# High parts subtracted in PSUM by TensorE, and two bias loads issued later, in a hybrid attention and expert layer

## The reference

```
gu = xe @ w_gu[e] + b_gu[e]                    # 1024 -> 2048
gate = min(gu[..., 0::2], 7); up = clip(gu[..., 1::2], -7, 7)
act = (up + 1.0) * (gate * sigmoid(gate * 1.702))
y = act @ w_dn[e] + b_dn[e]                    # 1024 -> 1024
out[row] += y * row_gate
```

## Time and profile before

| | |
|---|---|
| runs | 1425.9, 1427.1, 1428.12 us; median 1427.1 |
| profiled execution | 1428.16 us, span 1426.5 us |
| busy over the span | TensorE 93%, weight load 74%, VectorE 89%, ScalarE 72%, GpSimd 31% |
| transfers | 472.83 MB, mean 331 GB/s |
| TensorE clock | 0.99 of full speed over the span |

### The profile page before, as it was taken

One profiled execution on the slowest core, in us unless ns is written; L12 is line 12 of the kernel. 1 busy time (PEld: TensorE's weight loads), 2 busy tenths in 40 slices (PEclk: granted clock), 3 DMA queues, 4 the chain that ended last, 5 costly groups with the idle time before them and its releaser, 6 DMA issues.

```text
span 1426.5 us, 20070 instructions
## 1 busy us (share of the span) xinstructions
PE 1331.1 (93%) x6410; PEld 1058.9 (74%) x6410; DVE 1276.3 (89%) x1246; ACT 1026.1 (72%) x945; POOL 439.6 (31%) x286
## 2 busy tenths in 40 slices
PE   6999989898999999999999999999999999999996
PEld 5876866776877777787877777777878777788883
DVE  7448665689999999999999999999999999999998
ACT  5344444447788888878788888888787888877772
POOL 0000000023143536253444435362535444311100
PEclk9999999999999999999999999999999999999998
DMA  9511130279999999999999999999999999999994
GB/s 352 192 59 60 35 133 31 83 264 382 378 395 403 402 393 406 409 403 405 406 406 400 402 394 404 397 401 406 403 398 400 408 397 396 390 380 374 364 372 178
DMA packets 85573, 472.83 MB, mean 331 GB/s; under 512 B 16619, under 2 KB 16659, under 8 KB 34336
## 3 DMA queue, kind: packets, MB, share of 16 engines
q1 hardware_dynamic: 70736, 451.79, 79.6%
q0 software_dynamic: 14800, 20.55, 4.1%
HBM read 467.80 MB, written 22.02 MB: 343 GB/s over the span
## 4 chain that ended last, share of the span: by engine, by line
PE 50%; DVE 22%; issue 13%; DMA 7%; ACT 6%; POOL 0%; DVEq 0%; SPq 0%; POOLq 0%; ACTq 0%
DVE w_lo L1004 11%; PE gu_bank L1536 10%; PE gu_bank L1538 9%; PE gu_bank L1537 9%; DMA raw<-in_w_down_dram 5%; ACT w_hi L645 4%; PE turn_bank L1536 3%; PE turn_bank L1537 3%; PE turn_bank L1538 3%; DVE arena L1384 2%; PE bank L1536 1%; PE bank L1538 1%; PE bank L1537 1%; PE bank L1861 1%; DVE arena L1394 1%
## 5 line engine op out<-in xcount | busy, mean ns | idle before, releaser
L1004 DVE TENSOR_TENSOR w_lo<-raw,w_hi 128x2048 fp32r<-128x2048 f32 x409 | 916.4, 2283 | 61.1 <-ACT w_hi L645 60.1
L645 ACT ACTIVATE w_hi<-raw 128x2048 fp32r<-128x2048 f32 x409 | 771.9, 1921 | 120.7 <-PE gu_bank L1538 96.2
L610 POOL DMA_INDIRECT expert_rows<-arena x32 | 215.9, 6747 | 303.7 <-ACT arena L831 147.7
L1536 PE MATMUL gu_bank<-w_hi,turned 128*128 128x512 f32 x624 | 246.6, 395 | 3.8 <-DVE w_lo L1004 3.7
L1538 PE MATMUL gu_bank<-w_hi,turned 128*128 128x512 f32 x624 | 243.3, 390 | 0.0
L1537 PE MATMUL gu_bank<-w_lo,turned 128*128 128x512 f32 x624 | 243.1, 390 | 0.0
L1542 PE MATMUL gu_bank<-w_hi,turned 128*128 128x512 f32 x448 | 180.0, 402 | 29.2 <-DVE w_lo L1004 27.9
L1543 PE MATMUL gu_bank<-w_lo,turned 128*128 128x512 f32 x448 | 175.1, 391 | 0.0
L1536 PEld LDWEIGHTS gu_bank<-w_hi,turned 128*128 128x128 f32 x624 | 117.2, 188 | 33.6 <-DVE w_lo L1004 6.6
L584 POOL COPY arena<-arena 128x1 int32 (+1 forms) x32 | 53.0, 1657 | 285.7 <-PE bank L1854 275.1
L1538 PEld LDWEIGHTS gu_bank<-w_hi,turned 128*128 128x128 f32 x624 | 117.1, 188 | 24.8
(11 more groups left out here) (343 smaller groups left out, 1786.4 us busy)
## 6 DMA issues: line engine op xcount, KB each, us to landing
raw<-in_w_gate_up_dram SPq DMA_DIRECT2D x264, 1024.0 KB, 9.5
raw<-in_w_down_dram SPq DMA_DIRECT2D x132, 1024.0 KB, 8.4
raw<-in_w_in_dram SPq DMA_DIRECT2D x10, 1024.0 KB, 7.2
raw<-in_w_out_dram SPq DMA_DIRECT2D x4, 1024.0 KB, 5.1
raw<-expert_rows SPq DMA_DIRECT2D x4, 1024.0 KB, 6.5
turned<-split_biases POOLq DMA_DIRECT2D x132, 4.0 KB, 6.7
raw<-in_w_mem_kv_dram SPq DMA_DIRECT2D x2, 1024.0 KB, 12.5
arena<-in_x_dram SPq DMA_DIRECT2D x1, 2048.0 KB, 13.9
```

The costliest lines, as they stand in the source:

```text
L610: pool.indirect_dma_start(y_dram, bass.IndirectOffsetOnAxis(idx_scatter, 0), y_row, None, bounds_check=TOPK * S - 1, oob_is_err=False).the ...
L645: a.activation(home, raw_ap, ACT.Copy).then_inc(hi_ready, halves)
L1004: v.tensor_tensor(home[1], raw_ap, home[0].bitcast(F32), ALU.subtract).then_inc(lo_ready, halves)
L1536: pe.matmul(bank, a[0], b[0], start=first, stop=False)
```

## The change

Two things change. The loads of `g_final` and `b_dn` are issued on GpSimd's queue after the pairs, where the loop is split in two at `LOOP_FROM`. And in the pairs the low part of turned rows comes about in another way: after ScalarE has copied the high part, TensorE adds (-identity) x high part to the bank, in place, and ScalarE copies what is left. `low_act` and `low_x` are these copies, `rest_of_acts` and `rest_of_x` the matmuls; VectorE's subtractions leave the pair's steps. The matmuls stand after the fourth gate and up half (activations) and after the first down half (rows of the next block). The transposes get other start flags, since a bank is added to afterwards. `low_act` is as `low_x` with `la`, `ha`, `act_rest` and `alo_ready`; `rest_of_acts` as `rest_of_x` with `ha`, `act_rest` and a wait for `ahi_ready` of n * 2 + 1. In the steps with narrow gate and up halves both stand at the same places with 128 rows, and VectorE's `turn_act` and `turn_x` are taken out there too. The steps in which only wide blocks meet are as before.

```
@@ pool
-            pool.dma_start(g_final, final_norm_g.unsqueeze(0).to_broadcast([P, D])).then_inc(gf_in, 16)
-            for t in range(NT):
-                pool.dma_start(b_dn[t * E:(t + 1) * E, :], b_down[0]).then_inc(gf_in, 16)
...
+            steps(2, LOOP_FROM)
+            pool.dma_start(g_final, final_norm_g.unsqueeze(0).to_broadcast([P, D])).then_inc(gf_in, 16)
+            for t in range(NT):
+                pool.dma_start(b_dn[t * E:(t + 1) * E, :], b_down[0]).then_inc(gf_in, 16)
+            steps(LOOP_FROM, loops)
@@ scalar
+            def low_x(n, rows=P):
+                low = lx[:, :, :] if rows == P else hx[:, :, NARROW_ROWS:P]
+                a.wait_ge(x_rest, n)
+                for q in range(2):
+                    ks = slice(4 * q, 4 * q + 4)
+                    a.activation(low[:, ks, :], turned_rows[:, ks, 0:rows], ACT.Copy).then_inc(xlo_ready, 1)
...
+            a.activation(minus_one, ident, ACT.Copy, scale=-1.0)
@@ scalar, wide_after_narrow
                 turn_act_narrow(1, b)
-                for i in range(7, 12):
+                hi_m(GU + 7, b)
+                low_act(b, NARROW_ROWS)
+                for i in range(8, 12):
                     hi_m(GU + i, b)
                 sigmoid(b + 1)
...
-                for i in range(12, 16):
+                hi_m(GU + 12, b)
+                low_x(b, NARROW_ROWS if narrow_next else P)
+                for i in range(13, 16):
@@ scalar, narrow_after_wide
                 turn_act(1, b)
-                for i in range(7, 11):
+                hi_m(GU + 7, b)
+                low_act(b)
+                for i in range(8, 11):
...
                 hi_m(GU + 12, b)
+                low_x(b)
                 sigmoid(b + 1, NARROW_ROWS)
@@ vector, wide_after_narrow and narrow_after_wide
-                turn_act_narrow(0, b * 2)
-                turn_act_narrow(1, b * 2 + 1)
...
@@ tensor
+            def rest_of_x(n, rows=P):
+                pe.wait_ge(xhi_ready, n * 2 + 4)
+                for q in range(2):
+                    ks = slice(4 * q, 4 * q + 4)
+                    ins = pe.matmul(turned_rows[:, ks, 0:rows], minus_one, hx[:, ks, 0:rows], start=False, stop=True,
+                                    skip_group_check=True)
+                ins.then_inc(x_rest, 1)
...
@@ tensor, wide_after_narrow
                     if k == 2:
                         turn_acts(b)
+                    if k == 3:
+                        rest_of_acts(b, NARROW_ROWS)
...
                 for j in range(DN):
                     down(j, 2 * GU + j, b, narrow=True)
+                    if j == 0:
+                        rest_of_x(b, rows_next)
```

More of the change, by code:

```diff
@@ L283, in hymba_layer @@
         ha, la = (R[:, i * D:(i + 1) * D].rearrange("p (k s) -> p k s", k=KT) for i in (2, 3))
+        minus_one = R[:, 7 * D:7 * D + P]
         ones_r = R[:, 7 * D + P:7 * D + 2 * P]
@@ L620, in _, with steps @@
             bias_of_block(1)
[L621 to L625, removed]
+            def steps(first, end):
+                with pool.Fori(first, end) as b:
+                    pool.wait_ge(xtp_done, b + 1)
+                    gather(bass.ds(b + 1, 1), b * 2)
+                    bias_of_block(b)
+                    scatter(b - 2, b * 2 + 1)
+            steps(2, LOOP_FROM)
[3 more added lines that the diff above has]
+            steps(LOOP_FROM, loops)
             pool.wait_ge(xtp_done, loops + 1)
@@ L815, in turn_act_narrow, with low_act @@
                              ACT.Copy).then_inc(ahi_ready, 1)
+            def low_x(n, rows=P):
[4 more added lines that the diff above has]
+                    a.activation(low[:, ks, :], turned_rows[:, ks, 0:rows], ACT.Copy).then_inc(xlo_ready, 1)
+            def low_act(n, rows=P):
+                low = la[:, :, :] if rows == P else ha[:, :, NARROW_ROWS:P]
+                a.wait_ge(act_rest, n)
+                for q in range(2):
+                    ks = slice(4 * q, 4 * q + 4)
+                    a.activation(low[:, ks, :], turned_rows[:, ks, 0:rows], ACT.Copy).then_inc(alo_ready, 1)
             def low_of_gate_up(n):
@@ L1450, in wide_after_narrow @@
                 lo_m(GU + 11, b)
[L1451 to L1455, removed]
                 activate(b + 1, b)
@@ L1477, in _ @@
             with v.Fori(1, NARROW) as n:
-                wide_after_narrow(n * 2, True)
+                wide_after_narrow(n * 2)
                 narrow_after_wide(n * 2 + 1, n + 1)
-            wide_after_narrow(LOOP_FROM - 2, False)
+            wide_after_narrow(LOOP_FROM - 2)
             wide_after_wide(LOOP_FROM - 1)
@@ L1853, in turn_rows, with rest_of_acts @@
                 for k in range(KT):
-                    ins = pe.transpose(psum[6 + k // 4][:, k % 4 * P:(k % 4 + 1) * P],
-                                       h_row[:, k * P:(k + 1) * P], ident)
+                    ins = pe.matmul(psum[6 + k // 4][:, k % 4 * P:(k % 4 + 1) * P], h_row[:, k * P:(k + 1) * P], ident,
+                                    start=k % 4 == 0, stop=True, is_transpose=True, skip_group_check=True)
                 ins.then_inc(xtp_done, 1)
+            def rest_of_x(n, rows=P):
+                pe.wait_ge(xhi_ready, n * 2 + 4)
+                for q in range(2):
+                    ks = slice(4 * q, 4 * q + 4)
+                    ins = pe.matmul(turned_rows[:, ks, 0:rows], minus_one, hx[:, ks, 0:rows], start=False, stop=True,
+                                    skip_group_check=True)
+                ins.then_inc(x_rest, 1)
+            def rest_of_acts(n, rows=P):
+                pe.wait_ge(ahi_ready, n * 2 + 1)
+                for q in range(2):
+                    ks = slice(4 * q, 4 * q + 4)
+                    ins = pe.matmul(turned_rows[:, ks, 0:rows], minus_one, ha[:, ks, 0:rows], start=False, stop=True,
+                                    skip_group_check=True)
+                ins.then_inc(act_rest, 1)
             def turn_acts(n):
@@ L1860, in turn_acts @@
                 for k in range(KT):
-                    ins = pe.transpose(psum[6 + k // 4][:, k % 4 * P:(k % 4 + 1) * P],
-                                       act_by_slice[:, k, :], ident)
+                    ins = pe.matmul(psum[6 + k // 4][:, k % 4 * P:(k % 4 + 1) * P], act_by_slice[:, k, :], ident,
+                                    start=k % 4 == 0, stop=True, is_transpose=True, skip_group_check=True)
                 ins.then_inc(atp_done, 1)
@@ L1934, in narrow_after_wide @@
                         turn_acts(b)
+                    if k == 3:
+                        rest_of_acts(b)
                 gu_bias(b, narrow=True)
@@ L1942, in narrow_after_wide @@
                         fold_gate_up(n)
+                        rest_of_x(b)
             pe.wait_ge(sig_half, 1)
@@ L1950, in _ @@
                 narrow_after_wide(b, n + 1)
-            wide_after_narrow(LOOP_FROM - 2)
+            wide_after_narrow(LOOP_FROM - 2, P)
             wide_after_wide(LOOP_FROM - 1, NARROW)
```

14 lines of the change are left out of this document (3 added, 11 removed).

## The result

The changed kernel takes 1468.54 us (median of five runs, 1467.43 to 1471.75) against 1426.46 us: ratio 1.0299, 95% interval 1.0286 to 1.0312. The forecast had the sign and the waits, 27 us more; measured are 42, outside the range of 1438 to 1465 us. The profiled execution took 1471.75 us.

What follows compares the result with a forecast made beforehand. It took the bound to alternate within a 65.12 us pair, TensorE in wide halves, VectorE in narrow. Fourteen pairs at +2.06 give 28.8, less 0.8 and 1.3: +26.7 us, 1454 us; own range 1446 to 1464, widened 1438 to 1465.

Steps and rivals of the forecast that it cites:

- place 1: Wide block, after first narrow down half: TensorE waits 2.46 us for x copies, subtracts for 0.33; down products end 2.79 later.
- rival (c): Worse: unpipelined subtractions take 0.39 us, plus 0.2 latency at each place; 2.1 us more a pair, 1484 (half: 1469); chance 0.06.
- Where the bound changes hands: Inside a pair, TensorE is the slower in the 12 wide halves (2.72 us each), VectorE in the 12 narrow (2.21).
- place 2: Narrow block, after fourth gate and up half: stall 0.63 us plus subtractions, next half +1.95; gate and up end +1.15.
- place 4: Wide gate and up: no stall, 0.23 us of work less 0.2 for a small gap; +2.06 at next wide block.
- place 3: Narrow block, after first wide down half and the fold: stall 0.32 us, subtractions 0.57; shift of +2.04.
- The four places: Points in a pair where TensorE's subtraction must wait for a ScalarE copy; together a pair grows by 2.06 us to 67.2.
- rival (a): Second and third stalls vanish because ScalarE reaches its copies in time: a pair grows only 1.1 us, 1441 us; chance 0.12.
- That relief of VectorE shortens neither chain: Narrow stretch: two chains of about one length; taking 4.1 us a pair of subtractions off VectorE shortens neither.
- Rival (b): Faster: VectorE is the bound and its relief pulls everything up; 1414 us, or 1392 with all gaps gone; chance 0.09.
- the transfers keep up: Long stretch of pairs: ScalarE hardly ever waits for weights, 11.6 us in 980.
- The loads moved: Norm row and bias loads issued later: weights up to 2.9 us earlier in the first narrow block; 1.3 us gain taken.

Runs made afterwards that it cites:

- e3: Changed kernel with the first matmul of the narrow down products done eight times over ahead of its turn in wide blocks, filling TensorE's wait: 1451.71 us, ratio 1.0178.
- e2: Changed kernel with the subtraction of the next block's rows moved in wide blocks from behind the first narrow down half to behind the third: 1468.41 us, ratio 1.0284.
- e6: Kernel before, with only the next block's rows in wide blocks subtracted by TensorE, high and low copies ahead of ScalarE's sigmoid: 1425.88 us, ratio 1.0001.
- e9: Kernel of e6 with gate and up transfers of blocks 1 and on bringing 1792 of 2048 columns: 1412.73 us, ratio 0.9908 to the kernel before.
- e4: Changed kernel with the next block's row copies, high and low, put ahead of the sigmoid on ScalarE in wide blocks: 1438.12 us, ratio 1.0072.
- e10: Kernel before with gate and up transfers of blocks 1 and on bringing 1792 of 2048 columns, as control: 1423.17 us, ratio 0.9975.
- e1: Kernel before with only the norm row and down bias loads moved behind the pairs: 1426.64 us, ratio 0.9996.
- e12: Kernel of e3 with two more matmuls in place of eight, so the wait is half filled: 1468.81 us, ratio 1.0302 to the kernel before.
- e7: Changed kernel with VectorE subtracting from the activations again, TensorE only from the next block's rows: 1454.62 us, ratio 1.02.
- e11: Changed kernel with gate and up transfers of blocks 1 and on bringing 1792 of 2048 columns: 1469.91 us, ratio 1.0309.
- e5: Kernel before with the high copies of the next block's rows ahead of the sigmoid on ScalarE in wide blocks, VectorE still subtracting: 1426.4 us, ratio 0.9999.
- e8: Changed kernel with VectorE subtracting from the next block's rows again, TensorE only from the activations: 1432.45 us, ratio 1.0045.

## Why the prediction missed

**The failed step is place 1 of the sum**: "TensorE stands for 2.46 us, then 0.33 for the two subtractions: the down products end at 655.57". The wait was right (2.47 us by the pace), the pace behind it wasn't: I carried 0.227 us a matmul on through it. At the lower clock the subtractions take 0.59 us together and the next six matmuls 0.43 each in the pair shown; it is 1.6 us more in 9 of 13 pairs and 2.7 in the last. That is 17.1 us of the profiled execution's 43.5; e3 has a difference of the same size in the medians (1468.5 against 1451.7), and 1451.7 is near what the sum without the clock had forecast (1454). The step was a missing term: the price of the lower clock behind a wait stood neither in the sum nor in the range. The trace of before could have warned of it, by the granted 0.50 behind the wait of 1.53 us at 346.55, shown above; the waits in its 13 pairs, up to 1.47 us, had no fall behind them. The Trainium skill has the mechanism (TensorE: Matmul & The Clock Gate, section What's actually happening): the array gets its full clock only while it has been busy, else half. The trace agrees with the two levels, 1.00 and 0.50. Half of rival (c)'s price, 1469 us, is the measured time by luck: it had guessed 8 x 0.16 us for unpipelined subtractions, and no such thing was seen. Wherever the clock was full, two subtractions cost 0.57 us with 512 columns and 0.34 with 256 (723.20 to 723.54 in e3), as in the sum.

**Where the bound changes hands** held. TensorE's pace sets wide halves; N to W is 37.05 us, +1.0 on the 36.05 of the pair that the forecast was carried through, for its +0.91. The sum has small slips: under place 2, 0.65 and a restart of 0.1 taken from 1.95 leave 1.20, not 1.15, and under place 4 the gap of 0.05 with its restart is 0.15, not 0.2. The first changes nothing behind it, since at place 3 TensorE goes on where ScalarE's copy ends; the second is worth 0.7 us in all.

**The four places.** By the pace, place 1 waited 2.47 us (2.46 predicted), place 2 0.57 (0.63), place 3 0.23 (0.32), place 4 none (none). So rival (a), that the waits of places 2 and 3 vanish, doesn't hold.

**That relief of VectorE shortens neither chain** held in this order: VectorE's busy time in a pair fell from 63.89 to 60.97 us and nothing came of it. e2 showed ScalarE's chain by itself. In another order it doesn't hold (e6 and e9). Rival (b), faster, fails on the order in e4 (no faster than before even with the rows' wait gone) and has a second obstacle that I had not weighed: e6 and e9 show that transfers hold a pair near 65.3 us on average. The prediction's "the transfers keep up" was true of the kernel before (fewer bytes give it only 3 us, e10), but a pair much shorter than 65 us wasn't to be had with these bytes.

**The loads moved**: 1.3 us forecast; none was measured (e1), but so small a gain can't be told from none.

What stays open: why the clock falls in 9 of 13 pairs and not in the other 4, whose wait is the same (2.31 or 2.32 us). The trace narrows it down to when the wait comes. The falls in these pairs begin at 458.33, 594.87, 663.13, 731.40 us and so on, 68.27 us apart or twice that, while the waits come 67.1 or 68.6 us apart and so drift against them. In e2, where a pair takes 68.3 us, every pair has its fall. What sets these instants isn't shown. And e1 to e12 contain no version that beats the kernel before with all its work done: e6 equals it.

## What to carry to other kernels

An accumulating or subtracting matmul that needs another engine's result stalls everything queued behind it, so before moving work onto TensorE look at what stands ahead of the copy that releases it; here one sigmoid ahead of the rows' copies cost 30 of 42 us. Price a long TensorE wait (1.9 us was enough in most pairs of e12) as the wait plus the slower matmuls behind it, and consider doing harmless work in it. And freeing a 98%-busy engine pays only if the next chain and the transfers are not already as long: carry all of them through one period before counting on it.

## What the runs showed of the hardware

Behind waits of 1.87 to 2.4 us the granted TensorE clock was 0.50 for about 3 us: in 9 of 13 pairs for the wait of 2.31 us (the changed kernel, e7, e11), in 10 for that of 1.87 us (e12), and in all 13 in e2, whose fold waited 2.42 us after an earlier wait of 0.75. In these pairs the fall began between 0.4 us before and 1.4 us after the matmuls resumed, so most of the wait is recorded at 1.00. Behind the two waits of e4 (0.54 and 1.63 us) no stretch from W to N was longer than 28.87 us.

The length of the wait alone doesn't decide. The last pair of the kernel before has a wait of 2.15 us (at 1243.42) without a fall, and so has e1; e5, e8 and e10 have that wait with one. The last pair's wait of 2.8 us had a fall in the changed kernel and e7 and none in e11. And the first narrow block of the kernel before had one behind a wait of 1.53 us, with one of 1.28 us 3.6 us earlier.

Redundant matmuls made a kernel 17 us faster (e3). And a transfer stream at a DMA share of 1.00 and some 400 GB/s gave little sign of being a bound in the kernel before, 11.6 us of waits and some stretches from N to W up to 0.5 us longer, until another edit tried to shorten the pair by 1%.
